# One-core encoder trunk: linear-attention scratch laid out by chunk, query stores issued from ScalarE, rotary queries stored once, the two states of a head stacked on partition halves

## What is computed

```python
def step(state, inp):                       # gla_scan, one direction, chunk by chunk
    b = jnp.cumsum(gc, axis=2)
    o = att @ vc + (qc * jnp.exp(b)) @ state
    state = jnp.exp(b_last)[..., None] * state + (kc * jnp.exp(b_last - b)).T @ vc
o = rms_norm((o_f + o_b), g_norm) * silu(z)  # forward and backward scan are added

q = (rms_norm(cq, g_q) @ w_uq).reshape(B, S, 4, 128 + 64)
qn, qr = q[..., :128], apply_rope(q[..., 128:], cos, sin)
s = qn @ kn.T + qr @ kr.T                   # softmax attention over blocks of 128 queries
```

## Time and profile before

| | us |
|---|---|
| median of 3 runs (2978.84 to 2982.73) | 2980.94 |
| the profiled execution | 2989.56 |
| its span, first to last instruction | 2987.8 |
| PE busy in the span | 2878.2 |
| the joint stage, 590 to 760 us: PE / DVE / ACT / POOL busy | 146.7 / 116.5 / 108.2 / 85.5 |

### The profile page before, as it was taken

One profiled execution on the slowest core, in us unless ns is written; L12 is line 12 of the kernel. 1 busy time (PEld: TensorE's weight loads), 2 busy tenths in 40 slices (PEclk: granted clock), 3 DMA queues, 4 the chain that ended last, 5 costly groups with the idle time before them and its releaser, 6 DMA issues.

```text
span 2987.8 us, 48655 instructions
## 1 busy us (share of the span) xinstructions
PE 2878.2 (96%) x15972; PEld 2394.4 (80%) x15972; DVE 1611.9 (54%) x2749; ACT 1363.7 (46%) x2458; POOL 1141.9 (38%) x1118
## 2 busy tenths in 40 slices
PE   4999999988999999999999999999999999999998
PEld 4768888777788888887887888878887888888887
DVE  6567777766677777774335222255557555532111
ACT  4652254566455555553236111256556656532111
POOL 0211111245233333332330763177676767623221
PEclk8999999989999999999999999999999999999999
DMA  7243355487211111112652332342335332244231
GB/s 266 72 125 104 104 161 163 160 280 234 71 59 58 56 57 56 56 56 90 212 186 102 140 146 84 102 134 95 102 103 183 105 102 95 93 166 158 94 103 56
DMA packets 285737, 357.65 MB, mean 120 GB/s; under 512 B 20196, under 2 KB 190308, under 8 KB 285063
## 3 DMA queue, kind: packets, MB, share of 16 engines
q1 hardware_dynamic: 282536, 344.43, 35.3%
q0 software_dynamic: 3072, 11.54, 0.9%
HBM read 241.99 MB, written 113.90 MB: 119 GB/s over the span
## 4 chain that ended last, share of the span: by engine, by line
PE 84%; DVE 4%; issue 4%; ACT 4%; DMA 2%; POOL 2%; SPq 0%; DVEq 0%; ACTq 0%; POOLq 0%
PE PS L2999 6%; PE PS L3007 6%; PE PS L3003 6%; PE PS L2358 4%; PE PS L2359 4%; PE PS L2360 4%; PE PS L342 4%; PE PS L344 4%; PE PS L343 4%; PE PS L1779 4%; PE PS L1757 4%; PE PS L2526 4%; PE PS L2527 3%; PE PS L2528 3%; PE PS L1780 2%
## 5 line engine op out<-in xcount | busy, mean ns | idle before, releaser
L342 PE MATMUL PS<-hTh,whi 128*128 128x512 f32 x640 | 257.9, 403 | 1.5 <-DVE hTl L296 1.1
L2999 PE MATMUL PS<-hTh,wc 128*128 128x512 f32 x896 | 243.6, 394 | 8.9 <-DVE zu L2933 6.1
L344 PE MATMUL PS<-hTh,wlo 128*128 128x512 f32 x640 | 250.6, 392 | 0.0
L343 PE MATMUL PS<-hTl,whi 128*128 128x512 f32 x640 | 250.3, 391 | 0.0
L2755 POOL TENSOR_TENSOR wc<-wpr,wc 128x512 fp32r<-128x512 f32 x128 | 176.3, 1377 | 181.4 <-ACT wc L2751 181.4
L1860 ACT ACTIVATE pb__164<-PS,nm,rq 128x512 f32<-128x512 f32 x256 | 197.1, 779 | 101.7 <-DVE nm L1923 101.4
L3003 PE MATMUL PS<-hTh,wc 128*128 128x512 f32 x896 | 240.5, 390 | 0.0
L3007 PE MATMUL PS<-hTl,wc 128*128 128x512 f32 x896 | 239.9, 390 | 0.2 <-DVE hTl L2699 0.2
L2358 PE MATMUL PS<-ow_h,of_h 128*128 128x512 f32 x576 | 224.2, 389 | 1.4 <-DVE oy L2309 1.4
L2360 PE MATMUL PS<-ow_h,of_l 128*128 128x512 f32 x576 | 224.1, 389 | 0.0
L2359 PE MATMUL PS<-ow_l,of_h 128*128 128x512 f32 x576 | 224.1, 389 | 0.0
(11 more groups left out here) (303 smaller groups left out, 7113.7 us busy)
## 6 DMA issues: line engine op xcount, KB each, us to landing
wpr<-wuz SPq DMA_DIRECT2D x128, 256.0 KB, 3.4
projT<-pev SPq DMA_DIRECT2D x80, 256.0 KB, 2.7
xt<-x SPq DMA_DIRECT2D x8, 2048.0 KB, 8.1
mw<-wmod SPq DMA_DIRECT2D x64, 256.0 KB, 2.8
oxt<-x SPq DMA_DIRECT2D x32, 512.0 KB, 4.6
sg_v<-vev SPq DMA_DIRECT2D x64, 256.0 KB, 2.4
vm<-sg_v SPq DMA_DIRECT2D x32, 512.0 KB, 3.9
sgT<-mT SPq DMA_DIRECT2D x32, 512.0 KB, 3.5
```

The costliest lines, as they stand in the source:

```text
L342: pe.matmul(PS[:, bank, :], w[1][:, s, k, :], hTh[:, k, b], start=(k == 0), stop=False)
L343: pe.matmul(PS[:, bank, :], w[1][:, s, k, :], hTl[:, k, b], start=False, stop=False)
L344: mm = pe.matmul(PS[:, bank, :], w[2][:, s, k, :], hTh[:, k, b], start=False, stop=(k == KD - 1))
L2999: pe.matmul(o, wc[:, k, 0, kk, :], h_tile(hTh, k, kk), start=(kk == 0 and not onto), stop=False, skip_group_check=onto)
```

## The change

Scratch. `cumT` and the K, Q, V and Z tiles of `projT` become one tensor `chnk` of 16 chunks, each with 16 slots of 128 columns on each partition. The 48 stores of those projection tiles and the 16 of `gcum` write four pieces of 512 bytes on each partition, in place of one of 2 KB. A chunk's decays, keys and queries are read in one DMA of 4 KB on each partition (before: two DMAs in pieces of 512 bytes), `m_z` in pieces of 2 KB; the loads of the level and backward parts read the same bytes from `chnk`.

States. For each head parity e a tile half holds the forward state and the other half the backward state (`m_sc`, three buffers). `qf` is 64 partitions of forward and 64 of backward query, so `outputs` has two products for each head. DVE makes `qf` and the state in four instructions of half the size each, and fills the first buffer with two memsets and two copies; SP loads the backward state in two DMAs of 64 partitions (`main_states`). POOL's two memsets of `qf` go.

Queries. `nope_store` is issued by ACT, behind `squares`. Rotary queries are stored once (`q_rot`, 16 DMAs), and the attention's query load becomes three DMAs in place of one (64 loads).

```diff
         def proj_store(sp, j):
-            sp.dma_start(projT[g, :, tb * 512:(tb + 1) * 512], pev[:, j % 2, :]).then_inc(s_pst[j % 2], 16)
+            if g in C_SLOT:
+                dst = chnk[4 * tb:4 * tb + 4, :, C_SLOT[g], :].rearrange("t p c -> p t c")
+                sp.dma_start(dst, pev[:, j % 2, :].rearrange("p (t c) -> p t c", t=4)).then_inc(s_pst[j % 2], 16)
+            else:
+                sp.dma_start(projT[g, :, tb * 512:(tb + 1) * 512], pev[:, j % 2, :]).then_inc(s_pst[j % 2], 16)
...
         def gates_store(sp, i):
-                sp.dma_start(cumT[n, :, tb * 512:(tb + 1) * 512], gcum[:, u, :]).then_inc(s_gst, 16)
+                sp.dma_start(chnk[4 * tb:4 * tb + 4, :, C_CUM + n, :].rearrange("t p c -> p t c"),
+                             gcum[:, u, :].rearrange("p (t c) -> p t c", t=4)).then_inc(s_gst, 16)
...
         def main_fk(sp, t):
+            sp.dma_start(m_in[t % 4].rearrange("p a b d c -> p (a b d) c"), chnk[t, :, C_CUM:C_V, :]).then_inc(s_ml[t % 4], 16)
...
+        def main_states(sp, t):
             sp.wait_ge(s_bss[(NT - 1 - t) % 2], 16 * ((NT - 1 - t) // 2 + 1))
+            for e in range(2):
+                sp.dma_start(m_sc[t % 3][HALF[1 - e], e].rearrange("p h v -> p (h v)"), gla_vs[t, HALF[e], GH * DV:]
+                             ).then_inc(s_msl[t % 3], 16)
...
                 if 1 <= t <= NT:
                     squares(t - 1)
+                if t >= 2:
+                    nope_store(act, (t - 2) // 4, (t - 2) % 4)
                 if t and t + 1 < NT:
                     main_factors(act, t + 1)
...
+                    dve.tensor_tensor(qf[t % 2][r, e], m_kq[s][r, :, 1], m_x[t % 2][r, 0], ALU.mult).then_inc(s_mqf, 1)
+                    dve.tensor_tensor(qf[t % 2][q, e], m_kq[s][r, :, 1], m_x[t % 2][r, 1], ALU.mult).then_inc(s_mqf, 1)
...
                 for p in range(2):
+                    for e in range(2):
+                        r = HALF[e]
+                        dve.scalar_tensor_tensor(m_sc[(t + 1) % 3][r, e, p, :], m_sc[t % 3][r, e, p, :], gtot[r, p, t:t + 1],
+                                                 PS[r, 7, p * DV:(p + 1) * DV], ALU.mult, ALU.add).then_inc(s_ms, 1)
...
-                    pe.matmul(o, qf[t % 2][:, 0, h, :], m_st[:, t % 2, h // 2, :], start=False, stop=False)
-                    mm = pe.matmul(o, qf[t % 2][:, 1, h, :], back, start=False, stop=True)
+                    mm = pe.matmul(o, qf[t % 2][:, h % 2, h // 2, :], m_sc[t % 3][:, h % 2, h // 2, :], start=False, stop=True)
```

More of the change, by code:

```diff
@@ L53 @@
 N_TILES = 20
+C_CUM, C_KQ, C_V, C_Z = 0, 4, 8, 12
+C_SLOT = {**{T_GK + n: C_KQ + n for n in range(4)}, **{T_GV + n: C_V + n for n in range(4)},
+          **{T_GZ + n: C_Z + n for n in range(4)}}
 NPAIR = N_TILES // 2
@@ L959, in emit @@
         M0 = H0
-        m_fe = [at("m_fe%d" % s, M0 + 8 * s * K, [P, 2, 2, P]) for s in range(4)]
-        m_kq = [at("m_kq%d" % s, M0 + (8 * s + 2) * K, [P, 2, 2, P]) for s in range(4)]
+        m_in = [at("m_in%d" % s, M0 + 8 * s * K, [P, 2, 2, 2, P]) for s in range(4)]
+        m_fe = [m_in[s][:, 0] for s in range(4)]
+        m_kq = [m_in[s][:, 1] for s in range(4)]
         attT = [at("attT%d" % s, M0 + (8 * s + 4) * K, [P, GH, P]) for s in range(4)]
         m_z = [at("m_z%d" % s, M0 + o * K, [P, GH, P]) for s, o in enumerate((6, 14, 38, 53))]
-        m_vs = [at("m_vs%d" % s, M0 + (32 + 8 * s) * K, [P, GH * DV + 2 * DV]) for s in range(4)]
+        m_vs = [at("m_vs%d" % s, M0 + (32 + 8 * s) * K, [P, GH * DV]) for s in range(4)]
         m_x = [at("m_x%d" % p, M0 + (35 + 8 * p) * K, [P, 3, 2, P]) for p in range(2)]
@@ L968, in emit @@
         m_kf = at("m_kf", M0 + 51 * K, [P, 2, 2, P])
-        m_st = at("m_st", M0 + 30 * K, [P, 2, 2, DV])
+        m_sc = [at("m_sc%d" % j, M0 + o * K, [P, 2, 2, DV]) for j, o in enumerate((30, 66, 74))]
         m_kT = [at("m_kT%d" % p, M0 + (55 + 8 * p) * K, [P, 2 * P]) for p in range(2)]
         og = at("og", M0 + 59 * K, [P, 2, GH, P])
-        qf = [at("qf%d" % p, M0 + (64 + 8 * p) * K, [P, 2, GH, P]) for p in range(2)]
+        qf = [at("qf%d" % p, M0 + (64 + 8 * p) * K, [P, 2, 2, P]) for p in range(2)]
         ocol = at("ocol", M0 + 196 * K + 160, [P, 2, GH])
@@ L1108, in rope_store @@
                 c = (2 * r + h) * S + tb * 512
-                for half in range(2):
-                    sp.dma_start(q_all[1, half * ROPE:(half + 1) * ROPE, c:c + 512], rst[h * ROPE:(h + 1) * ROPE, r, :]
-                                 ).then_inc(s_qr[r], 16)
+                sp.dma_start(q_rot[:, c:c + 512], rst[h * ROPE:(h + 1) * ROPE, r, :]).then_inc(s_qr[r], 16)
         def lat_sp(sp, t):
@@ L1401, in main_sp @@
             load(2)
+            main_states(sp, 2)
             level_store(sp, NU - 1)
@@ L1415, in main_sp @@
                     load(t + 4)
+                if t + 3 < NT:
+                    sp.wait_ge(s_mo, t + 1)
+                    main_states(sp, t + 3)
                 if t >= 2:
@@ L1422, in main_sp, with query_load @@
                     first_queries(sp)
+        def query_load(sp, u, tok):
+            sp.dma_start(qraw[:, u, 0, :], q_all[:, tok]).then_inc(s_qi[u], 16)
+            for half in range(2):
+                sp.dma_start(qraw[half * ROPE:(half + 1) * ROPE, u, 1, :], q_rot[:, tok]).then_inc(s_qi[u], 16)
         def first_queries(sp):
@@ L1469, in main_dve @@
             dve.wait_ge(s_pb, 8 + NBLK)
-            dve.memset(m_st[:, 0, :, :], 0.0).then_inc(s_gm, 1)
+            dve.wait_ge(s_bs, 2 * NT)
+            for e in range(2):
+                dve.memset(m_sc[0][HALF[e], e], 0.0).then_inc(s_gm, 1)
+                dve.tensor_copy(m_sc[0][HALF[1 - e], e], st[HALF[e], (NT - 1) % 2, :, :]).then_inc(s_gm, 1)
             dve.tensor_scalar(ggn[:, :], ggn[:, :], float(DK) ** -0.5, None, ALU.mult).then_inc(s_gm, 1)
-            dve.wait_ge(s_gm, 8)
+            dve.wait_ge(s_gm, 9)
             def q_states(t):
```

92 lines of the change are left out of this document (39 added, 53 removed).

## The result

The changed kernel takes 2995.78 us (median of 7 runs, 2991.54 to 3001.70), the kernel before, run beside it, 2982.73 us (7 runs, 2978.84 to 2991.10): ratio 1.0033, 95% interval 1.0019 to 1.0046, 10 us or a third of a per cent slower. The forecast was 2978, counted from a median of 2980.94 for the kernel before; the range ended at 2986. The profiled execution took 2997.29 us, its span is 2995.5.

The account below looks back on a forecast made before the run. PE was taken to bound the kernel overall, but a chain ACT, DVE, PE half of each joint-stage round. Round terms of -0.75, -2.17 and -0.13 gave -3.05 us from 2980.94, so 2978; range 2964 to 2986 for 8 in 10.

Parts of the forecast that it names:

- The reading of the stage: Joint stage: a chain ACT, DVE, PE sets half of every round; PE waits there, so shorter `outputs` does not shorten it.
- the sum: Chain terms of chunks 5 to 8, 9 to 12 and the last round: -0.75, -2.17, -0.13, together -3.05 us.
- matmuls less: `outputs` on PE, four fewer per chunk: 0.67, 1.63 and 1.16 us saved on the chain in the three rounds.
- `nst` stored by ACT: ACT's wait for the store ends, saving 1.64 and 2.10 us before DVE's mean; issuing costs ACT 0.50 us a round.
- state in four: DVE's state: four instructions take about 1.13 us for 0.61, so 0.53 us more, five times on the chain.
- `qf` in four: DVE's `qf` in four instructions: no change taken, the bound 0.3 us longer, seven times on the chain.
- Start of the stage: Two memsets and two copies for one memset: up to 1.3 us more on DVE, taken as zero within 1 us.
- Transfers: New stores, joint-stage loads, rotary stores and query loads: no added cost, zero on the chain or hidden by PE's work.
- The rival of the stores: Gates' stores land later, delaying scans and the first level: up to 18 us slower, 2996 at the worst; 8%.
- The rival of the clock: PE idles more, so n = 4 and n = 7 run slower, 1.2 us a group, seven times: 2986; 10%.

Follow-up runs that it names:

- 7: Changed kernel with DVE's order per chunk altered: state first, then the latent projection's ck, rsw and rst, `qf` last: 2983.89 us, 0.9998 to the kernel before.
- 6: Kernel before with only the state in four instructions on half the partitions, for two on all: 2993.06 us, ratio 1.0029.
- 4: Changed kernel with each head's first `outputs` matmul issued twice, so PE again has twelve per chunk: 2999.14 us, 1.0047 to the kernel before.
- 2: Kernel before with only the stores of `nst` issued by ACT in place of SP: 2981.57 us, ratio 0.9988.
- 3: Changed kernel with the stacking undone (twelve matmuls, `qf` and state in two instructions); new layout and ACT's `nst` stores stay: 2983.44 us, 0.9992 to the kernel before.
- 1: Kernel before with only DVE's instruction counts raised, `qf` and state in four each on half the partitions: 2997.66 us, ratio 1.0045.
- 12: Changed kernel with twelve extra 128x128 matmuls ahead of n = 4 and n = 7, keeping PE at work: 2994.15 us, 1.0029 to the kernel before.

## Why the prediction was wrong

*The reading of the stage was right.* The chain ACT, DVE, PE sets the pace of half of each round, PE's matmuls are not what it waits for there, and DVE's order alone is worth 10 us (7). By my own chain a longer DVE had to cost time. What failed is the pricing of DVE's instructions, and the clock behind PE's longer waits, which the sum had at nothing. In the traces, over the three rounds of the sum:

| term | predicted | changed against before |
|---|---|---|
| steps from 5, 9, 13: matmuls less | -3.46 | -4.45, clock of these steps included |
| `nst` stored by ACT | -3.74 + 1.50 | -3.9 |
| state in four, five times | +2.65 | +4.9 |
| `qf` in four, five times | 0 | +4.5 |
| n = 4 and n = 7 at the lower level, five times | 0 | +6.4 |
| rotary key work up to `rsw`, twice | 0 | +1.0 |
| the other four steps | 0 | +1.0 |
| together | -3.05 | +9.5 |

*State in four, +0.53 a chunk, five times on the chain: the step that failed.* I took four for 1.13 us from one of 0.34 and the overlap of two. Four took 1.48 us, with no overlap left, +0.88 in duration (0.98 start to start), and alone 1.0029 (6). Five times 0.98 is 4.9 us of the 9. In the trace of 6 the steps from chunks 7 and 11 grow by 3.4 and 3.5 us, and their n = 7, behind waits of 4.78 and 5.20 us, runs at the lower level, which before it did not; how the rest splits this run does not tell.

*`qf` in four, "no change", bound +0.3: failed too.* I set four undisturbed instructions (4 x 0.43 = 1.71 us) against a pair beside POOL's work (1.82). Like with like, the second chunk's four take 1.81 us start to start (605.30 to the state at 607.11), the pair there 1.41 to 1.44, +0.37 to 0.40; over the 13 chunks from the fourth on, beside POOL's work, the mean to the next instruction is 2.60 for 1.85, +0.75 (2.21 to 3.25). The rule that I weighed and set aside, the Trainium skill's "VectorE: DVE Perf Modes", "The TRN2 errata", had this right in sign and nearly in size: 0.31 for the measured 0.37 to 0.40, and its 424 ns stand against 0.41 to 0.42 us in the rows. The rule has no term for the stretches of 0.72 to 1.15 us. All of these lie beside POOL's instructions (nearly as many of 0.42 us do too), and in 7, where `qf` stands elsewhere, the mean falls from 551 and 639 ns to 425 and 443. That POOL causes them is what this suggests; no run changed POOL alone.

*Four matmuls less, -3.46 us in three rounds.* Right in place and nearly in size: the steps from 5, 9 and 13 fell by 0.78, 2.53 and 1.14 us for the 0.67, 1.63 and 1.16 predicted. The middle one is partly luck: before, part of its one-column products ran at the lower level too (0.89 to 0.99 us a row of four, 0.58 in the changed kernel). What the sum lacks is that the clock took it back elsewhere (4).

*`nst` from ACT, -3.74 + 1.50.* The mechanism was right, and so were the places: 1.71 and 2.18 us went for the 1.64 and 2.10 predicted. The issue was over-priced. It lies beside `osq`, and the factors start 0.59 us behind `osq` where without it they start 0.48 behind, so it costs 0.11, not 0.50 (ACT before, then ACT and its queue in the changed kernel, in order of time).

```profile
711.05 0.59 ACT L1443 ACTIVATE osq<-PS 128x512 f32<-128x512 f32 x1
711.53 0.42 ACT L1370 ACTIVATE m_x<-m_fe 128x256 f32<-128x256 f32 x1
```

```profile
681.57 0.59 ACT L1456 ACTIVATE osq<-PS 128x512 f32<-128x512 f32 x1
681.70 0.34 ACTq L1111 DMA_DIRECT2D q_all<-nst  x1
682.16 0.42 ACT L1375 ACTIVATE m_x<-m_in 128x256 f32<-128x256 f32 x1
```

Measured alone it gave -3.6 us (2), against -2.24 in the sum and -3.74 without the issue.

*Start of the stage, 0 within 1.* Two memsets and two copies took 1.36 us (595.70 to 597.06), near the 1.3 I had as the bound. None of it reached the end: DVE's second mean comes at 620.03 us before and 620.04 after, because its wait for `osq` there shrank from 6.58 to 2.65 us. The 2.8 us that chunk 4 is late arise behind that, in the first round's `qf`, state and products, which had no term in the sum.

*Transfers, 0.* Right: 3 against 2, and the `gcum` wait. *The rival of the stores* is refuted with it. Its estimate of 0.4 us took the row pitch of the Trainium skill's "DMA: Bandwidth & Descriptors", "Latency and other measured facts", for the 1 MiB between a partition's four pieces; in `chnk` the rows of neighbouring partitions lie 8 KiB apart. The stores of `gcum` landed in 2.2 to 4.1 us, median 2.5, for 2.4 to 3.5, median 2.8.

*The rival of the clock* named the right mechanism with the right price, 1.2 us a group (1.25 measured), for six of the seven groups, one of which had it before too. What it said against itself, that "after the 3.03 us gap n = 7 still ran fast", held before; of the seven longer waits now, 3.04 to 4.18 us, one was followed by full speed. Its trigger, a PE with less to do, can only be part of it: with twelve matmuls and a slower DVE (1) four of seven groups are slow, with twelve in the changed kernel (4) three, with eight six.

*The rotary key work*, +0.52 us twice, had no term, and no run isolates it. The measured terms add up to the +9.5 us of these rounds in the traces because they are cut out of the same traces; that they come near the 10 us of the medians too is a check on the size, with the first round's 2.8 us and what is regained behind the stage nearly cancelling.

## What to carry to other kernels

Halving the partitions of an instruction saved nothing here (346 ns for 64x128, 345 for 128x128): an edit that removes matmuls by making DVE's instructions smaller and twice as many has to be charged the full time of each new one, counted at the engine that the stage waits for. Where a chain of engines sets the pace, the order of the slow engine's work is the cheaper lever: moving `qf` and the rotary part within DVE's order gave 0.6%, some 18 us, on the stacked kernel (1.0033 to 0.9973), with no work removed; on the unstacked one it gave 0.26% (0.9992 to 0.9966), and `qf` alone nothing. And a wait of PE that grows can cost twice, once as the wait and once as the lower clock of what follows, here 1.25 us for a group of six products.

## Not expected of the hardware

- Two state instructions of 128x128 in a row overlap (0.60 us for two of 0.345); four of 64x128, alternating between the partition halves, do not (1.48 us for four of 0.346). Four in another order of the halves were not run.
- A DMA issued from ACT cost ACT 0.11 us: 0.34 us on its queue, beside the activation ahead of it, and the next activation 0.59 us behind that one for 0.48.
- The length of a wait alone doesn't tell which level follows. Behind a wait of 2.63 us PE was at the lower level (12), behind one of 3.02 at full speed (before), behind one of 3.04 at the lower again (changed kernel, at 758.47), and behind all of 3.84 to 4.18 at the lower. With PE kept at work ahead of n = 4 and n = 7 (12), n = 4 ran at full speed, and the one-column products of n = 0, 20 us ahead of it in the round, at the lower level.
